# A hybrid decoder block on one core: routing beside the mix product, expert weights in loads of 4 MiB, and a rotation over 16 places

## The chip, the cores and the metric

The kernel runs on one core of a Trainium2 chip. The metric is device time in microseconds (us) for one execution, lower being better; what is compared are medians of several executions. The profiled execution is one more, and it has a time of its own.

## The reference, cut to what matters

A token mixer (a gated convolution beside chunked retention, 16 meta tokens ahead of 256 real ones) is followed by a mixture of experts: 32 experts, 4 for each token. `EXPERT_BLOCK` is only how the reference pads; each expert has 8 MiB of `w_gate_up` and 4 MiB of `w_down` in float32.

```python
h = h + token_mixer(rmsnorm(h, norm_mix_w), ...)      # ends in: merged @ w_mix_out
xn = rmsnorm(h, norm_ffn_w)
logits = xn @ w_router + b_router                     # 256 x 32
top_v, top_i = lax.top_k(logits, 4)
gates = softmax(top_v)
def expert(xb, e):                                    # for the tokens that chose e
    hgu = xb @ w_gate_up[e] + b_gate_up[e]            # 1024 -> 2048
    g, u = min(hgu[:, :1024], 7), clip(hgu[:, 1024:], -7, 7)
    return (g * sigmoid(1.702 * g) * (u + 1)) @ w_down[e] + b_down[e]
h = h + sum of gates * expert outputs
out = rmsnorm(h, norm_final_w)[:, 16:]
```

## The kernel before

**Stages.** The five engines run hand-written streams, tied by semaphores; there is no scheduler. Up to about 394 us of the profiled execution the token mixer runs: products with `w_in` in split precision (L500 to L502), with `w_ret_out` (L582) and `w_conv_out` (L484). Then come the product with `w_mix_out` (L605, `yret` times the ring's units), the second norm, the router (L618), and the choice of experts. From 452 us on the experts run, one block of up to 64 token slots at a time; with these inputs there are 32 blocks, one per expert. `last` and `rounds` are read from `nblocks`, a table that DVE works out (`further_blocks`).

**Routing before.** The mix product goes through its four column units `n`, with both token halves `t` in each. As each pair of units ends, DVE adds it to the residual `hx`. When all four are in, ACT squares both halves (L906), POOL makes the inverse roots (L438), DVE writes the normed tokens `xn2` (L1226), and TensorE transposes them (L462), ACT copies them from PSUM to `xn2T` (L912), and TensorE multiplies by the router `wr`. DVE takes the maxima, their indices, a mask and (after products with `before` and `ones`) the rank of each token at its expert, in `slot`. The tokens of a block are gathered by a product with a one-hot matrix. That product is in bfloat16; so that nothing is lost, the tokens are split in three parts, `x3` (ACT writes a part, L909, L916, L921; DVE subtracts it and leaves the rest, L1231, L1257). The gather (L634) makes `xT`, the block's tokens with the model dimension on the partitions. Eight products with the identity (L718) put `hx` in PSUM banks 0 to 3, where the experts' outputs are added up.

**A block.** Its weights are 12 units of 1 MiB: eight of `w_gate_up` and four of `w_down`. The order on TensorE is: `hidden(1)` with units 4 to 7 of gate_up, the gather for the next block, the scatter of the block before (L707), `down(0)` with two units of w_down (L683), `hidden(0)` of the next block with its units 0 to 3, `down(1)` with the last two. `hidden` is L662, and L655 is its bias, which comes first. Each unit that has been used adds one to `w_used`: 4 after the first `hidden(0)`, 12 more for each block.

**Loads.** SP issues them all, in one queue. The first four units have places of their own in `split_w` and are never loaded again; the other twelve places (`pair_w`, `rT`, two parts of `ring`, `scratch`) are taken in pairs, 2 MiB for each load, in rows of 16 KB per partition. `pair` (L328) loads one; `reload` waits until both units of the place have been used:

```python
sp.wait_ge(w_used, LOADS * b + (n + AHEAD + 2))
pair(n, e, of, j)
```

In all, 16 MiB are loaded ahead of the first expert product, some of it while the token mixer runs: 6 MiB at 304 us, 2 at 368, and the rest from 396 on; the last pair waits for the router and for `x3`.

## Time and profile before

| | |
|---|---|
| median of 3 executions | 1382.29 us (1381.57 to 1383.05) |
| the profiled execution | 1390.49 us, span 1388.7 us, mean granted clock 0.987 |
| busy share of the span | PE (TensorE) 93%, DVE 39%, ACT 19%, POOL 1% |
| the chain that ended last | PE 51%, DMA 43%, of which rT<-in_w_gate_up 42% |
| moved | 467.78 MB, mean 337 GB/s over the span |

The span runs from the first to the last instruction of the profiled execution. Shares of busy time are means over stages that differ: in the second half of the span all 16 DMA engines are busy as well. PEld is TensorE's loading of weights, which overlaps PE. A float32 product shows as two records.

### The profile page before, as it was taken

Reading aid. Unit: us, or ns where it says so; the run is one execution under the profiler, and the core shown is the slowest. Engines: PE = TensorE matmul, PEld = TensorE weight load, DVE = VectorE, ACT = ScalarE, POOL = GpSimd, SP = SyncE. Lnnn points to the kernel's source line nnn. Section 1 sums busy time; section 2 is a strip of 40 time slices with the busy share of each in tenths; the row PEclk is TensorE's granted clock in tenths of the full one; section 3 lists DMA queues with packets and bytes.
Section 4 is the critical chain, followed back from the end, with each engine's and each line's share of the span. In section 5 each row is a group of like instructions: output and inputs, shape, how many; then the busy total and the mean of one; then the engine's idle time right before and its main releaser. Section 6 shows DMA issues by size and latency. Waiting matters only on the chain.

```text
span 1388.7 us, 21351 instructions
## 1 busy us (share of the span) xinstructions
PE 1292.2 (93%) x8375; PEld 720.2 (52%) x8375; DVE 538.9 (39%) x1070; ACT 260.3 (19%) x468; POOL 13.5 (1%) x29
## 2 busy tenths in 40 slices
PE   4999999999997999999999999999999999999996
PEld 4998899898886334333333333333333333333332
DVE  5797898851214423232322223223222222232231
ACT  5554443420103111111111101101111111011011
POOL 1000000000000000000000000000000000000000
PEclk9999999999997999999999999999999999999998
DMA  9653443456661699999999999999999999999994
GB/s 305 219 162 122 150 151 130 144 200 225 210 245 61 236 430 429 427 429 429 429 427 429 429 429 428 428 429 429 428 428 429 429 428 429 429 429 428 428 429 201
DMA packets 89374, 467.78 MB, mean 337 GB/s; under 512 B 5647, under 2 KB 63543, under 8 KB 64679
## 3 DMA queue, kind: packets, MB, share of 16 engines
q1 hardware_dynamic: 88112, 465.27, 82.3%
q10 hardware_dynamic: 1239, 2.20, 0.6%
q8 instruction: 14, 0.23, 0.1%
q14 instruction: 9, 0.07, 0.0%
HBM read 466.41 MB, written 1.05 MB: 337 GB/s over the span
## 4 chain that ended last, share of the span: by engine, by line
PE 51%; DMA 43%; DVE 2%; ACT 2%; issue 1%; ACTq 0%; SPq 0%; DVEq 0%; POOL 0%
DMA rT<-in_w_gate_up 42%; PE pb L662 15%; PE pb L500 6%; PE pb L502 6%; PE pb L501 6%; PE pb L683 5%; PE pb L582 4%; PE pb L605 2%; PE pb L484 2%; PE pb L462 1%; ACT ubuf L932 1%; PE pb L618 1%; PE pb L674 1%; PE pb L568 0%; DMA hx<-in_x 0%
## 5 line engine op out<-in xcount | busy, mean ns | idle before, releaser
L683 PE MATMUL pb<-ring,ubuf 128*64 128x512 f32 x1008 | 230.2, 598 | 19.1 <-ACT ubuf L932 14.7
L1346 DVE TENSOR_SCALAR scratch<-pb 64x512 f32<-64x512 f32 x64 | 43.7, 682 | 472.6 <-PE pb L662 472.6
L500 PE MATMUL pb<-parts,whi 128*128 128x256 f32 (+1 forms) x640 | 187.0, 292 | 5.6 <-DVE parts L1005 5.6
L502 PE MATMUL pb<-parts,wlo 128*128 128x256 f32 (+1 forms) x640 | 183.6, 287 | 0.0
L501 PE MATMUL pb<-parts,whi 128*128 128x256 f32 (+1 forms) x640 | 183.6, 287 | 0.0
L662 PE MATMUL pb<-rT,ubuf 128*64 128x512 f32 x512 | 118.2, 604 | 28.4 <-DMA rT<-in_w_gate_up 28.4
L683 PEld LDWEIGHTS pb<-ring,ubuf 128*64 128x64 f32 x1008 | 66.8, 136 | 140.7 <-issue 107.9
L500 PEld LDWEIGHTS pb<-parts,whi 128*128 128x128 f32 x640 | 122.2, 191 | 8.9 <-issue 8.9
L501 PEld LDWEIGHTS pb<-parts,whi 128*128 128x128 f32 x640 | 121.9, 190 | 1.5 <-issue 1.5
L502 PEld LDWEIGHTS pb<-parts,wlo 128*128 128x128 f32 x640 | 122.1, 191 | 0.0
L662 PE MATMUL pb<-pair_w,ubuf 128*64 128x512 f32 x512 | 116.4, 596 | 0.0
L662 PE MATMUL pb<-scratch,ubuf 128*64 128x512 f32 x496 | 111.7, 592 | 0.0
L662 PE MATMUL pb<-ring,ubuf 128*64 128x512 f32 x496 | 111.7, 592 | 0.0
L992 DVE TENSOR_TENSOR wlo<-ring,whi 128x1024 fp32r<-128x1024 f32 x80 | 97.5, 1220 | 22.9 <-ACT whi L806 22.8
L806 ACT ACTIVATE whi<-ring 128x1024 fp32r<-128x1024 f32 x80 | 84.2, 1057 | 108.4 <-PE pb L502 104.8
L1036 DVE SCALAR_TENSOR_TENSOR scratch<-ubuf,par,scratch 128x256 f32<-128x256 f32 x232 | 97.4, 478 | 0.0
L662 PEld LDWEIGHTS pb<-rT,ubuf 128*64 128x64 f32 x512 | 35.1, 138 | 110.0 <-issue 61.3
L928 ACT ACTIVATE scratch<-scratch 64x512 f32<-64x512 f32 x64 | 39.9, 624 | 269.8 <-DVE scratch L1346 269.8
L932 ACT ACTIVATE ubuf<-pb 128x256 f32<-128x256 f32 x64 | 24.6, 384 | 314.0 <-PE pb L672 314.0
L662 PEld LDWEIGHTS pb<-ring,ubuf 128*64 128x64 f32 x496 | 35.6, 137 | 70.8 <-issue 70.8
L662 PEld LDWEIGHTS pb<-pair_w,ubuf 128*64 128x64 f32 x512 | 34.8, 137 | 71.3 <-issue 58.0
L707 PE MATMUL pb<-ubuf 64*128 64x512 f32 x264 | 65.6, 615 | 0.9 <-ACT ubuf L944 0.9
(212 smaller groups left out, 1143.9 us busy)
## 6 DMA issues: line engine op xcount, KB each, us to landing
ring<-in_w_down SPq DMA_DIRECT2D x63, 2048.0 KB, 21.9
pair_w<-in_w_gate_up SPq DMA_DIRECT2D x32, 2048.0 KB, 25.5
rT<-in_w_gate_up SPq DMA_DIRECT2D x32, 2048.0 KB, 25.5
scratch<-in_w_gate_up SPq DMA_DIRECT2D x31, 2048.0 KB, 22.7
ring<-in_w_gate_up SPq DMA_DIRECT2D x31, 2048.0 KB, 24.1
ring<-in_w_in SPq DMA_DIRECT2D x40, 1024.0 KB, 5.1
ring<-in_w_ret_out SPq DMA_DIRECT2D x8, 1024.0 KB, 5.0
split_w<-in_w_gate_up SPq DMA_DIRECT2D x2, 2048.0 KB, 10.1
```

Source lines behind the costliest of these rows:

```text
L500: pe.matmul(o, wh, xh, start=first, stop=False)
L501: pe.matmul(o, wh, xl, start=False, stop=False)
L502: ins = pe.matmul(o, wl, xh, start=False, stop=last)
L582: ins = pe.matmul(pb[:, 2 * (f % 2) + j, 0:REAL], ring[:, s, k % KC, j * P:(j + 1) * P], rT[:, VC + k, :], start=(k == 0), stop=(k == 2 * ...
L662: ins = pe.matmul(pb[u * SLOTS:(u + 1) * SLOTS, bank, :], xT[:, 2 * i + k, :], w[:, k, u * HID:(u + 1) * HID], start=False, stop=(i == 3 a ...
L683: ins = pe.matmul(pb[c * SLOTS:(c + 1) * SLOTS, 6, :], actT[:, s, 2 * i + k, :], w[:, k, c * HID:(c + 1) * HID], start=False, stop=(s == 1 ...
L707: ins = pe.matmul(pb[:, 2 * t + c, :], hotT[rows, t * P:(t + 1) * P], ysb[rows, :], start=False, stop=stop, skip_group_check=True)
L806: sc.activation(whi[:, 2 * (u % 2) + c, :], m_raw(u, c), ACT.Copy).then_inc(m_hi, 1)
L928: sc.activation(sig, hg, ACT.Sigmoid, scale=ALPHA).then_inc(sig_rdy, 1)
L992: dve.tensor_tensor(wlo[:, 2 * (u % 2) + c, :], m_raw(u, c), whi[:, 2 * (u % 2) + c, :].bitcast(F32), ALU.subtract).then_inc(m_lo, 1)
L1036: ins = dve.scalar_tensor_tensor(out=acc if w < TAPS - 1 else cv[:, 2 * i + j, :], in0=u, scalar=tap, in1=acc, op0=ALU.mult, op1=ALU.add)
L1346: dve.tensor_scalar(hg, pb[0:SLOTS, 4 + s, :], LIMIT, None, ALU.min).then_inc(min_rdy, 1)
```

## The change

There are two parts.

**The routing.** The mix product now goes through the first token half for all four units, and then through the second. While it is at the second half, the first is added to the residual, multiplied by the norm's weight (into a new buffer `hw`, without the inverse root), transposed, and multiplied by the router; the inverse root is applied to the logits instead. The choice for the first half is made there as well. The first block's gather no longer uses the three bfloat16 parts: it is a float32 product of `hw` with `hot1`, for each half, into banks 5 and 7. The three parts, the identity products and the block table are still made, and stand behind the first block's gather.

On TensorE, at the end of the mix product, before (each pair of rows is one token half; L462 the transposes, L618 the router, L624 to L628 the ranks, L634 the gather, L718 the identity products, L655 the first expert product's bias):

```order
L605 MATMUL pb<-ring,ubuf 128x256 x15
L462 MATMUL pb<-ident,ubuf 128x128 [waits xn_done]
...
L462 MATMUL pb<-ident,ubuf 128x128 [waits xn_done]
...
L618 MATMUL pb<-scratch,ring 128x32 [waits x2e,rout_in]
...
L618 MATMUL pb<-scratch,ring 128x32 [waits x2e]
...
L624 MATMUL pb<-scratch,before 128x32 [waits lgt_read,route]
...
L634 MATMUL pb<-onehot,scratch 128x64 [waits hot_rdy,x3_rdy]
L634 MATMUL pb<-onehot,scratch 128x64 x47
L718 MATMUL pb<-hx,ident 128x512 [waits h2_done]
L718 MATMUL pb<-hx,ident 128x512 x3
...
L655 MATMUL pb<-bias,pick_e 64x512 [waits xt_rdy,sel_rdy,zeroed,b3_step]
```

And now, from the transposes of the first half on (L475 transposes, L644 the mix product, L620 the router, L657 and L666 ranks, L630 the float32 gather, L706 the bias):

```order
L475 MATMUL pb<-ident,hw 128x128 [waits hw_done]
...
L644 MATMUL pb<-work,ubuf 128x256 [waits landed4]
...
L620 MATMUL pb<-work 128x32 [waits x2e,rout_in]
...
L620 MATMUL pb<-work 128x32 [waits x2e]
...
L644 MATMUL pb<-work,ubuf 128x256 [waits landed5]
...
L657 MATMUL pb<-work,before 128x32 [waits h2_done,route]
L475 MATMUL pb<-ident,hw 128x128 [waits hw_done]
...
L620 MATMUL pb<-work 128x32 [waits x2e]
...
L630 MATMUL pb<-hot,hw 128x64 [waits hot_rdy,xf_rdy]
...
L630 MATMUL pb<-hot,hw 128x64 [waits hot_rdy,xf_rdy]
...
L706 MATMUL pb<-bias,pick_e 64x512 [waits xt_rdy,sel_rdy,zeroed,b3_step]
```

The transposes and the router of the first half stand ahead of the mix product's last unit; the three-part gather and the identity products are gone from ahead of L706. They stand right behind the first four units instead:

```order
L713 MATMUL pb<-split_w,ubuf 64x512 [waits e_in0]
...
L713 MATMUL pb<-split_w,ubuf 64x512 [waits e_in0]
L713 MATMUL pb<-split_w,ubuf 64x512 x3
L772 MATMUL pb<-hx,ident 128x512 [waits h2_done,table_done]
L772 MATMUL pb<-hx,ident 128x512 x3
L775 TENSOR_LOAD nblocks [waits x3_rdy]
L775 ISA x2
L776 TENSOR_LOAD nblocks
L776 ISA x2
...
L706 MATMUL pb<-bias,pick_e 64x512 [waits clip_rdy,min_rdy]
```

Before, L727's load of `last` followed there alone. Now two waits, the identity products (L772) and two register loads stand between the first `hidden(0)` and block 0's `hidden(1)`, whose bias is the last row.

On DVE, in what it does between the second rank and the first block's tokens, before (L1257 subtracts the second part, L1259 is `slot`, L1262 the one-hot, L1298 writes `xT`):

```order
L1254 TENSOR_REDUCE scratch<-scratch 128x32 [waits route_step]
L1257 TENSOR_TENSOR ring<-ring,scratch 128x2048 [waits x3_rdy]
L1259 SCALAR_TENSOR_TENSOR scratch<-pb,scratch 128x64 [waits rank_done]
L1262 TENSOR_SCALAR onehot<-iota_s,scratch 128x64 [waits route_step]
L1262 TENSOR_SCALAR onehot<-iota_s,scratch 128x64
...
L1303 MEMSET scratch 64x512 [waits gathered]
L1304 MEMSET scratch 64x512
L1298 COPY ubuf<-pb 128x512 [waits gathered]
...
L1269 TENSOR_SCALAR scratch<-pb 128x32
```

And now (L1393 and L1396 write `xT`, L1405 subtracts a part, L1359 begins the block table):

```order
L1321 TENSOR_REDUCE work<-work 128x32 [waits route_step]
L1327 SCALAR_TENSOR_TENSOR work<-pb,work 128x32 [waits rank_done,route]
L1329 TENSOR_SCALAR hot<-iota_s,work 128x64 [waits route_step]
...
L1393 COPY ubuf<-pb 128x512 [waits first_done]
L1396 TENSOR_TENSOR ubuf<-ubuf,pb 128x512 [waits gathered,half_done]
L1397 MEMSET work 64x512
L1398 MEMSET work 64x512
...
L1405 TENSOR_TENSOR hw<-hw,work 128x2048 [waits x3_rdy]
L1359 TENSOR_SCALAR work<-pb 128x32 [waits rank_done]
...
L1379 MEMSET off 128x32 [waits route_step]
L1405 TENSOR_TENSOR hw<-hw,work 128x2048 [waits xr_rdy,x3_rdy,route_step]
```

The subtractions of 2048 columns have moved behind `xT`, with the block table between them.

**The loads.** The parts of SBUF are laid out anew, so that 16 places of 1 MiB lie in four groups of four in a row. For the first 28 blocks (`FIXED`; expert and block have the same number there) the weights are loaded by `four`, 4 MiB at once, as 128 rows of 32 KB, and all four groups rotate, those of the first units too. The layout of the weights in memory is changed on the host to match. The last blocks are loaded in pairs of 2 MiB, as before, in the upper twelve places. TensorE's loop over blocks is written out four times, since the groups rotate by three for each block.

In SP's queue the first four loads of 4 MiB stand where the mixer still runs (at r = 3 and n = 2 of the loops over the ring's units), behind the merge, and behind the mix product. The fifth waits for four used units; the ones that follow wait for 8, 16, 14, 20, 28, 26, ... used units, in this order.

The core of the diff:

```diff
+            def four(i, e):
+
+                b = (i - 1) // 3
+                of, q, d = ((w_gu, 0, 0), (w_gu, 1, 0), (w_dn, 0, 0))[i % 3] if i else (w_gu, 0, 0)
+                x = e + (b + 1 if i % 3 == 0 else b) if i else 0
+                sp.dma_start(place_at(4 * (i % 4), 4), expert_src(x, of, q)).then_inc(e_in[i % 4], 16)
+
+            def used(i):
+
+                b = (i - 1) // 3
+                return LOADS * b + (14, 8, 16)[i % 3] if i else AHEAD
...
             sp.wait_ge(merged, KC)
+            four(2, 0)
+            sp.wait_ge(mix_done, 8)
+            four(3, 0)
...
+            sp.wait_ge(w_used, used(0))
+            four(4, 0)
+            with sp.Fori(0, trips) as g:
+                for i in range(5, 17):
+                    sp.wait_ge(w_used, 4 * LOADS * g + used(i - 4))
+                    four(i, 4 * g)
...
             def reload(b, n, e, of, j):
-                sp.wait_ge(w_used, LOADS * b + (n + AHEAD + 2))
-                pair(n, e, of, j)
+                sp.wait_ge(w_used, LOADS * b + (AHEAD + (FIXED - 1) * LOADS + max(n + 2, 12 if n == 8 else 0)))
+                later_pair(n, e, of, j)
...
+            hidden(0, first_unit, 0)
+            pe.wait_ge(table_done, 4)
             pe.wait_ge(h2_done, 4)
             for t in range(TT):
                 for c in range(2):
                     pe.matmul(pb[:, 2 * t + c, :], ident[:, :], hx[:, t, c * 512:(c + 1) * 512],
                               start=True, stop=False, skip_group_check=True)
+            pe.wait_ge(x3_rdy, PARTS + 1)
...
-    gu = w_gate_up[0].reshape(NE, 2, 2, 2, P, 2, 2, HID).transpose(0, 6, 1, 4, 2, 3, 5, 7).reshape(NE, 4, P, 4 * D)
-    dn = w_down[0].reshape(NE, 2, 2, 2, P, D).transpose(0, 1, 4, 2, 3, 5).reshape(NE, 2, P, 4 * D)
+    gu = w_gate_up[0].reshape(NE, 8, P, 2, 2, HID).transpose(0, 4, 2, 1, 3, 5).reshape(NE, 2, P, 8 * D)
+    dn = w_down[0].reshape(NE, 8, P, D).transpose(0, 2, 1, 3).reshape(NE, 1, P, 8 * D)
```

## Rows read from the trace of the kernel before

**Rows 1.** The page's second part: GB/s moved, in 40 equal slices of the span
```profile
GB/s 305 219 162 122 150 151 130 144 200 225 210 245 61 236 430 429 427 429 429 429 427 429 429 429 428 428 429 429 428 428 429 429 428 429 429 429 428 428 429 201
```

**Rows 2.** Two stretches: us, busy by engine, granted clock, DMA share, GB/s
```profile
25.00:45.00 20.00, 20.00 (x146) 20.00 (x145) 12.84 (x15) 7.87 (x11) 0.00 (x0) 1.00 1.09 348
500.00:1350.00 850.00, 795.49 (x5161) 308.07 (x5157) 227.30 (x471) 92.29 (x234) 0.00 (x0) 1.00 1.01 429
```

**Rows 3.** The chain that ended last, late: start us, us, what
```profile
1304.63 25.49 DMA rT<-in_w_gate_up
...
1330.16 3.68 PE pb L662 x16
...
1333.99 26.19 DMA rT<-in_w_gate_up
```

**Rows 4.** SP's queue, expert loads of 2 MiB: start us, us, instruction
```profile
444.87 0.34 SPq L328 DMA_DIRECT2D ring<-in_w_down  x1
463.02 0.35 SPq L328 DMA_DIRECT2D pair_w<-in_w_gate_up  x1
466.43 0.34 SPq L328 DMA_DIRECT2D rT<-in_w_gate_up  x1
474.96 0.33 SPq L328 DMA_DIRECT2D ring<-in_w_down  x1
...
487.15 0.33 SPq L328 DMA_DIRECT2D ring<-in_w_down  x1
...
494.23 0.33 SPq L328 DMA_DIRECT2D rT<-in_w_gate_up  x1
```

**Rows 5.** The chain between the mix product and the experts
```profile
438.84 0.20 DVE scratch L1244
...
440.62 2.21 DVE ring L1257
442.85 1.92 ACT scratch L921
...
447.56 4.40 PE pb L718 x8
451.96 0.34 PE pb L655 x2
...
459.16 0.22 PE pb L655 x2
```

**Rows 6.** TensorE in order of time; in brackets the idle time before
```profile
395.55 27.89 PE L605 MATMUL pb<-ring,ubuf 128*128 128x256 f32 x128 [1.03 <-DVE ubuf L1216]
...
427.97 0.89 PEld L462 LDWEIGHTS pb<-ident,ubuf 128*128 128x128 f32 x8 [4.92 <-DVE ubuf L1226]
427.97 1.28 PE L462 MATMUL pb<-ident,ubuf 128*128 128x128 f32 x8 [4.52 <-DVE ubuf L1226]
```

**Rows 7.** DVE and ACT by line and shape: busy us, mean ns, idle before
```profile
L1220 DVE TENSOR_TENSOR hx<-hx,pb 128x512 f32<-128x512 f32 x4 | 2.8, 688 | 25.9 <-PE pb L605 25.9
...
L912 ACT ACTIVATE ring<-pb 128x1024 f32<-128x1024 f32 x2 | 2.0, 1014 | 0.1
```

**Rows 8.** DVE around the block table, in order of time
```profile
447.72 0.48 DVE L1303 MEMSET scratch<- 64x512 f32 x1 [3.61 <-PE pb L634]
...
450.03 0.12 DVE L1269 TENSOR_SCALAR scratch<-pb 128x32 f32<-128x32 f32 x1
...
454.65 0.09 DVE L1289 MEMSET off<- 128x32 f32 x1
```

**Rows 9.** SP reading a register from SBUF: duration ns min/median/max
```profile
L385 SPq TENSOR_LOAD <-nblocks x1: 471/471/471, 452.9 to 452.9; - x1
```

**Rows 10.** A stretch of the router products, columns as in rows 2
```profile
432.15:435.57 3.42, 3.42 (x18) 3.42 (x18) 0.99 (x2) 3.04 (x3) 0.00 (x0) 0.50 0.00 0
```

**Rows 11.** The page's sixth part: KB each, us from issue to landing
```profile
ring<-in_w_in SPq DMA_DIRECT2D x40, 1024.0 KB, 5.1
ring<-in_w_ret_out SPq DMA_DIRECT2D x8, 1024.0 KB, 5.0
```

More of the change, by code:

```diff
@@ L42 @@
 AHEAD = 4
+PLACES = 16
+FIXED = 28
 HW = KC * UNIT // 2
@@ L352, in _ @@
                     sp.wait_ge(b_full, RET0)
-                    for n in range(0, AHEAD, 2):
-                        first_pair(n)
-                    pair(0, 0, w_gu, 4)
+                    four(0, 0)
                 load(LRET + 2 * r, w_ro[:, 0:KC, :], r)
@@ L363, in _ @@
                     sp.wait_ge(b_full, CONV0)
-                    pair(2, 0, w_gu, 6)
+                    four(1, 0)
                 load(LMIX + n, w_mo, n)
@@ L604, in _ @@
+            pe.wait_ge(a_free, 50)
+            for t in range(TT):
+                if t:
+                    pe.wait_ge(b_free, 50)
+                for n in range(UC):
+                    s, use = place(LMIX + n)
+                    pe.wait_ge(landed[s], 16 * use)
                     for k in range(KC):
-                        ins = pe.matmul(pb[:, n, t * UNIT:(t + 1) * UNIT], yret[:, k, t * P:(t + 1) * P],
+                        if t == 0 and n == 0 and k in (0, KC - 2):
+                            pe.wait_ge(merged, KC if k else KC - 2)
+                        ins = pe.matmul(pb[:, 2 * t + n // 2, n % 2 * UNIT:(n % 2 + 1) * UNIT], yret[:, k, t * P:(t + 1) * P],
@@ new lines, in _ @@
+            pe.matmul(pb[:, 0, 0:NE], before[:, :], mask[:, 0, :], start=True, stop=True).then_inc(rank_done, 1)
+            for half in range(2):
+                turn_h2(1, half)
+            pe.wait_ge(lgt_read, 1)
+            for half in range(2):
+                router(1, half)
+            gather_first(0, 5).then_inc(first_done, 1)
+            pe.matmul(pb[:, 1, 0:NE], ones[:, :], mask[:, 0, :], start=True, stop=False)
+            pe.wait_ge(route, 2)
+            pe.matmul(pb[:, 1, 0:NE], before[:, :], mask[:, 1, :], start=False, stop=True).then_inc(rank_done, 1)
```

346 lines of the change are left out of this document (195 added, 151 removed).

## The prediction

> **What bounds the kernel now.** Read first the rate of the weight loads over the span, slice by slice. From the second third on it stands at 427 to 430 GB/s and never moves [rows 1]; over 850 us the DMA engines are all busy, at 429 GB/s [rows 2]. Of the 32 experts' 384 MiB (12 MiB each: 402.7 MB), 16 MiB are fetched ahead of the first expert product and 368 MiB after it: 385.9 MB at 429 GB/s are 900 us. Then read the chain that ended last near its end: in each block it is a transfer of 25.5 us, some products of L662 (3.68), and the next transfer [rows 3]. A block takes 29.36 us there (1304.63 to 1333.99), which is 12.58 MB at 429 GB/s. Thirdly the queue of SP: early on, where TensorE sets the pace, the same place is loaded again after 27.80 us (466.43 to 494.23) [rows 4]. So TensorE needs 27.8 us a block, the loads 29.35, and the experts are bound by the loads once TensorE has used up what was fetched ahead. A TensorE saving within the experts is worth nothing; what counts is when the stream starts to run without a hole, and its rate.
>
> When does it start? The last load ahead is issued at 444.87 and is done some 5 us later; the next is issued at 463.02, as the sixth unit has been used [rows 4]. Two loads (2 MiB, 4.89 us each at 429 GB/s) fit between 463.02 and 474.96, where the next is issued; from there on each is issued before the one ahead of it is through. I call V the moment at which an unbroken stream would have had to begin: V = 474.96 - 2 x 4.89 = 465.2. The latency from issue to the first byte is the same in both kernels and drops out. The end of the kernel moves as V moves.
>
> **The routing.** Between the mix product's end at 423.44 [rows 6] and the first expert product's bias at 451.96 lie 28.5 us of chain: residual, squares, norm, transposes, router (L618), selection, a three-part copy of the tokens (2.21 on DVE at 440.62, 1.92 on ACT at 442.85), gather, and 4.4 us of identity products (L718) [rows 5]. The change puts half of it beside the product and takes out the rest, as the two orders show. Step by step:
> - The product (27.9 us from 395.55) starts when the convolution's last product is done and no longer waits for the last two `merged` chunks: the 1.03 us of idle ahead of it go [rows 6]. Into it go 8 transposes of the first token half (8 took 1.28 us at the full clock [rows 6]) and its 8 router products, 16 records. A load of 128x128 weights took 0.89/8 = 0.11 us [rows 6], so 1.8 us. End of the product: 423.4 - 1.0 + 1.3 + 1.8 = 425.5.
> - Behind it stay, for the second half only: residual of 512 columns 0.69 [rows 7] and the norm's weight at 512 columns, a quarter of L1257's 2.21 over 2048 [rows 5], 0.6; four transposes 0.6; ACT's copy of 512 columns, half of L912's 1.01 [rows 7], 0.5; four router products 0.9; the selection 1.6 (438.84 to 440.62 with one small operation moved out [rows 5]); rank and one-hot 0.8; eight float32 gather products, 16 records, 1.8; an add from PSUM 0.7; some 0.6 of semaphores. Sum 8.8: the first expert product at 434.3, 17.7 us earlier.
> - That is not yet the gain. Three things that stood ahead of the first product now stand behind it. The identity products come after it, and with them a wait for `x3_rdy`, that is for the three-part copy, and two register loads. The copy hangs on DVE: from 434.2 four memsets (0.48 or less each [rows 8]), a subtraction over 2048 columns (2.2 [rows 5]), the block table (450.03 to 454.74, 4.7 [rows 8]), a second subtraction 2.2, then ACT's last part 1.9 [rows 5], and 0.5 of semaphores: 434.2 + 1.8 + 2.2 + 4.7 + 2.2 + 1.9 + 0.5 = 447.5. The product of four units (6.9) and the identities (4.4) are done at 446, so TensorE waits. The two register loads took SP 0.47 and about 0.3, with checks 1.2 [rows 9]. So the second group of hidden products starts at 448.8. Queued behind it: everything of block 0, and through `w_used` the loads.
> - The clock. In the routing of before the granted clock was 0.50, with TensorE busy for a whole stretch on router products of 32 columns [rows 10]. The same thin products now stand in a tighter row. At half clock the router half and the gather (24 records) cost up to 24 x 0.11 = 2.6 more; if it stays full, nothing. I take 1.2: 450.0 against 459.16 before, 9.2 us earlier.
>
> **The loads.** 4 MiB at a time, 9.78 us each. SP waits for the first four units (441.5 to 445), one load; for eight units (457), one load, 9.8 us: through by 468. The third waits until the down units of block 0 are all used, as the group of four is freed only whole, 28.0 us after 450.0 (459.16 to 487.15 [rows 4, 5]): 478.0; the fourth goes with it. So the stream has a hole of some 10 us that it did not have in this size, and two loads of 4 MiB stand ahead of it. V' = 478.0 - 2 x 9.78 = 458.4. V moves by **-6.8 us**: of 17.7 us won in the routing, 8.5 go to what moved behind the first product, 2.4 to the coarser groups.
>
> Does it run dry later? The next group of the first half is freed at 478.0 + 7.1 and the queue lasts until 497.6; the next down group at 478.0 + 27.8 = 505.8, the queue lasts until 507.4 (it was given three loads): 1.6 us to spare, less the latency of an issue, and 1.5 more with each block. Once TensorE waits for loads, it waits for the next block's first group; it then frees the down group 12.2 us later (474.96 to 487.15 [rows 4]), with 19.6 us of loads behind: 7 us to spare. No second hole.
>
> **The rows.** At 25 to 45 us the loads had rows of 1 KB and ran at 348 GB/s with a busy share of 1.09; the experts' rows of 16 KB run at 429 with 1.01 [rows 2]. Per row an engine takes 16 x 1024 / (348/1.09) = 51 ns and 16 x 16384 / (429/1.01) = 617 ns; a straight line through both gives 14 ns per row and 603 per 16 KB. A row of 32 KB would then save 14 of 1234, 1.2%. 81 of the loads have it (340 MB, 792 us): 9.4 us. Rows of 1 KB may be slow for other reasons, and then the saving is nothing. I take half, **-4.8 us**. The Trainium skill, DMA: Bandwidth & Descriptors, section Bandwidth (Where 436 GB/s comes from), puts the fabric at 435 GB/s; by that alone the stream could gain at most 1.4%, and the 429 here agree with it as a ceiling.
>
> **The end.** The last four blocks are loaded in pairs as before. With lumps TensorE starts block 28's second pair of hidden units 12.2 + 3.4 = 15.6 us after the lump, they land 9.8 after it: 5.8 late. It wins back 1.55 in each of three blocks: **+1.1 us** remain. From the last load that TensorE waits for (1333.99 + 26.19) on, the tail is the same [rows 3].
>
> Sum -6.8 - 4.8 + 1.1 = -10.5 us. The profiled execution took 1390.49 with a span of 1388.7, 8.2 more than the median; the change in us carries over: 1382.3 - 10.5 = **1371.8**. The dense part up to 394 has the same instructions on TensorE, DVE and ACT, and no wait of TensorE for a load there; 4 MiB in place of 6 stand in the queue at 304.
>
> **Rivals.**
> 1. As above, the rows of 32 KB giving between 2 and 9 us: 1365 to 1376. Chance 0.50.
> 2. A row costs by its bytes alone. The line through two loads of unlike source and state is thin evidence. Then -5.7: 1376.6. Chance 0.25.
> 3. The first half of block 0 starts later than 450, by the clock falling through the first expert products too or by waits that I did not see in the chain of DVE and ACT. Each us costs one. From 456 on only the rows are left, near the time of before: 1379 to 1385. For it speaks how much the sum joins end to end; against it that the parts are all measured. Chance 0.15.
> 4. Slower: rows 32 KB apart lower the rate at which HBM delivers. 1% of 792 us is 7.9 us, so with nothing gained per row it decides from 1.1% (5.7 + 2.8 us); at 3% the time is 1400. Against it: the loads of w_in, with rows 40 KB apart, landed in 5.1 us, those of w_ret_out, 4 KB apart, in 5.0 [rows 11]. A 7 us margin at the down groups that is really used up would look the same. Chance 0.10. The Trainium skill, DMA: Bandwidth & Descriptors, section Latency and other measured facts, has copies slow down with row pitches that are large powers of two, from 512 KiB on; whether 32 KB rows come near it no run here shows.
>
> **The numbers.** A measurement of this kernel tells 0.2% (2.8 us) from no change. Best: clock full, 9.4 for the rows: -17, 1365. Bound of the others: block 0 at 453, rows nothing: -2.5, 1380. Range 1364.5 to 1380.0, which leaves out most of rival 4 and half of rival 3. Faster 0.84, same 0.06, slower 0.10.
>
> **What would show it.** In the profile after: the first L713 product at 434 to 437; a wait of TensorE for ACT (the copy to x3) ahead of the second group of hidden products, which starts near 450; one hole in the loads, some 10 us, ending near 478, and none after; a rate over 500 to 1250 of 430 to 433 GB/s (429: rival 2; less: rival 4); TensorE waiting for `split_w`, `late_w` or `work` loads once a block, from block 5 or so on. It would be wrong if the hole comes back in each block, or if TensorE's block takes over 29 us.

## The result, and the profile after

| | median, us | range, executions |
|---|---|---|
| before, beside it | 1382.76 | 1381.57 to 1386.55, 5 |
| changed | 1375.12 | 1374.32 to 1377.90, 5 |
| ratio | 0.9949 | 95% interval 0.9931 to 0.9966 |

The change is 7.6 us faster; in a later set, with its own executions of before beside it, 1376.17 against 1382.28 us, ratio 0.9958 (0.9938 to 0.9978). The forecast was 1371.8, 10.5 us faster, with a range of 1364.5 to 1380.0. The profiled execution of the changed kernel took 1375.12 us, its own median.

The page after: span, TensorE, GB/s in 40 slices, and the shares of the chain that ended last.
```profile
span 1373.1 us, 20662 instructions
PE 1282.8 (93%) x8359; PEld 719.0 (52%) x8359; DVE 540.5 (39%) x1075; ACT 262.6 (19%) x474; POOL 12.6 (1%) x29
GB/s 305 218 171 125 150 153 124 153 214 154 214 250 153 256 431 431 430 436 428 431 433 433 429 432 436 429 431 431 436 428 431 434 432 429 432 434 425 427 428 210
PE 63%; DMA 32%; ACT 2%; DVE 1%; issue 1%; ACTq 0%; SPq 0%; DVEq 0%
```
Against [rows 1] the plateau is some 3 GB/s higher, and the chain has moved from DMA (43%) to TensorE (51% to 63%): the last block that waits for a load ends that wait at 1247.66 us (1230.35 + 17.31 below), where in before it was at 1360.18 (1333.99 + 26.19 [rows 3]). The late chain after (start us, us, what):
```profile
1201.21 17.29 DMA late_w<-in_w_gate_up
1218.55 7.09 PE pb L713 x32
...
1226.65 3.68 PE pb L734 x16
1230.35 17.31 DMA split_w<-in_w_gate_up
1247.70 7.09 PE pb L713 x32
```
A block takes 1230.35 - 1201.21 = 29.14 us while the loads bound it, 29.36 before.

The product and the routing on TensorE after (start us, us, instruction, in brackets the idle time before):
```profile
417.52 3.70 PE L644 MATMUL pb<-work,ubuf 128*128 128x256 f32 x16
...
423.34 1.94 PE L620 MATMUL pb<-work 128*128 128x32 f32 x16
...
428.25 3.64 PE L630 MATMUL pb<-hot,hw 128*128 128x64 f32 x16 [0.74 <-DVE hot L1329]
...
433.32 0.64 PE L706 MATMUL pb<-bias,pick_e 128*64 128x512 bf16 x2 [0.62 <-DVE ubuf L1396]
433.72 9.08 PE L713 MATMUL pb<-split_w,ubuf 128*64 128x512 f32 x32
442.73 3.70 PE L772 MATMUL pb<-hx,ident 128*128 128x512 f32 x8
447.93 0.41 PE L706 MATMUL pb<-bias,pick_e 128*64 128x512 bf16 x2 [1.50 <-issue]
```
SP's queue of expert loads after, 4 MiB each:
```profile
300.81 0.34 SPq L327 DMA_DIRECT2D split_w<-in_w_gate_up  x1
...
442.83 0.33 SPq L327 DMA_DIRECT2D split_w<-in_w_gate_up  x1
455.42 0.35 SPq L327 DMA_DIRECT2D late_w<-in_w_down  x1
476.11 0.93 SPq L327 DMA_DIRECT2D work<-in_w_gate_up  x2
483.18 0.33 SPq L327 DMA_DIRECT2D split_w<-in_w_down  x1
503.92 0.33 SPq L327 DMA_DIRECT2D late_w<-in_w_gate_up  x1
```
Four stretches after (us, busy by engine, granted clock, DMA share, GB/s): the hole, the steady part, TensorE's clock in the routing, and an early one.
```profile
467.00:476.00 9.00, 8.53 (x45) 2.98 (x43) 2.74 (x4) 0.93 (x3) 0.00 (x0) 1.00 0.02 5
500.00:1250.00 750.00, 697.99 (x4551) 272.95 (x4553) 201.67 (x415) 81.87 (x208) 0.00 (x0) 1.00 1.00 432
427.60:437.80 10.20, 8.92 (x32) 5.90 (x34) 6.50 (x15) 1.19 (x5) 0.00 (x0) 0.50 0.48 208
21.00:28.00 7.00, 3.69 (x16) 3.70 (x17) 6.60 (x6) 4.21 (x4) 0.00 (x0) 0.53 1.07 338
```

**Two traces must be laid side by side with care.** The spans differ by 15.6 us, the medians by 7.6. The first expert load left SP's queue at 300.81 us here and at 304.39 in before, though nothing ahead of it on TensorE was changed. In before the granted clock was at half in these stretches, inside the long products:
```profile
118.00:121.50 3.50, 3.50 (x6) 1.42 (x7) 0.02 (x1) 0.00 (x0) 0.00 (x0) 0.52 0.90 298
254.70:258.10 3.40, 3.40 (x7) 1.50 (x6) 0.26 (x1) 0.00 (x0) 0.00 (x0) 0.50 0.89 299
```
After, it was at half (1.2 GHz instead of 2.4) at 21 to 28 us instead, where TensorE was busy for 3.69 of 7.0 us. Two times 3.4 us at half cost 3.4; that is the 3.58. It is not the change that did it: later traces of the changed dense part show both forms (the table below). So I add 3.58 us to every time of the changed trace before I set it against before's. What is left of 15.6 is 12.0 us: the start of the stream 4.9, its rate 5.7 (5.9 by the blocks), the rest 1.4.

All traces, by where the granted clock was at half ahead of 400 us, by the start of the first expert load, by the time at half clock in the routing, and by the span that is left behind the first expert load (all us):

| run | half clock ahead of 400 | first expert load | half clock in the routing | span behind that load |
|---|---|---|---|---|
| `before` | near 118 and 255 | 304.39 | 20.5 | 1084.3 |
| `before_again` | near 118 and 255 | 304.67 | 20.5 | 1084.9 |
| `before_third` | 20 to 31, near 164 | 303.26 | 17.1 | 1083.3 |
| changed | 21 to 28 | 300.81 | 10.2 | 1072.3 |
| `after_again` | 20 to 28 | 299.97 | 10.2 | 1072.2 |
| `pairs12` | 20 to 28 | 300.06 | 10.2 | 1076.6 |
| `rows16` | near 118 and 255 | 304.22 | 13.7 | 1080.1 |
| `rows8` | none | 300.47 | 17.1 | 1092.6 |
| `x3late` | near 118 and 255 | 304.38 | 13.7 | 1072.0 |
| `half6` | 20 to 28 | 299.86 | 10.2 | 1070.7 |
| `half6_x3late` | none | 300.58 | 17.1 | 1072.2 |
| `half3_x3late` | 21 to 29 | 300.97 | 10.2 | 1068.0 |
| `warm` | 20 to 28 | 300.10 | 10.2 | 1073.0 |
| `two_loads_32k` | 20 to 28 | 300.09 | 10.2 | 1899.1 |

The last column takes out the dense part, but not the clock in the routing.

### The profile page after: what moved, and what is told of

Read it like the earlier page. It is cut to its first block, busy times and chain, and to the rows that moved or that the text cites. A ratio compares the mean times of both kernels' runs of the same rounds, so it can differ in the third digit from the quotient of the medians.

```text
span 1373.1 us, 20662 instructions
## 1 busy us (share of the span) xinstructions
PE 1282.8 (93%) x8359; PEld 719.0 (52%) x8359; DVE 540.5 (39%) x1075; ACT 262.6 (19%) x474; POOL 12.6 (1%) x29
## 4 chain that ended last, share of the span: by engine, by line
PE 63%; DMA 32%; ACT 2%; DVE 1%; issue 1%; ACTq 0%; SPq 0%; DVEq 0%
PE pb L713 20%; DMA work<-in_w_gate_up 15%; PE pb L734 10%; DMA split_w<-in_w_gate_up 9%; DMA late_w<-in_w_gate_up 7%; PE pb L513 6%; PE pb L515 6%; PE pb L514 6%; PE pb L595 4%; PE pb L644 2%; PE pb L497 2%; ACT ubuf L1006 1%; PE pb L725 1%; PE pb L475 1%; PE pb L723 1%
## 5 line engine op out<-in xcount | busy, mean ns | idle before, releaser
L713 PE MATMUL pb<-work,ubuf 128*64 128x512 f32 x992 | 218.7, 593 | 13.3 <-DMA work<-in_w_gate_up 13.3
L1445 DVE TENSOR_SCALAR work<-pb 64x512 f32<-64x512 f32 x64 | 43.7, 683 | 467.3 <-PE pb L713 467.3
L713 PEld LDWEIGHTS pb<-work,ubuf 128*64 128x64 f32 x992 | 70.2, 137 | 147.4 <-issue 128.3
L734 PE MATMUL pb<-work,ubuf 128*64 128x512 f32 x576 | 131.5, 598 | 11.0 <-ACT ubuf L1006 8.5
L713 PE MATMUL pb<-late_w,ubuf 128*64 128x512 f32 x576 | 127.0, 593 | 6.2 <-DMA late_w<-in_w_gate_up 6.2
L713 PE MATMUL pb<-split_w,ubuf 128*64 128x512 f32 x480 | 107.9, 603 | 7.2 <-DMA split_w<-in_w_gate_up 7.2
L1066 DVE TENSOR_TENSOR wlo<-work,whi 128x1024 fp32r<-128x1024 f32 x80 | 97.5, 1221 | 21.8 <-ACT whi L861 21.8
L861 ACT ACTIVATE whi<-work 128x1024 fp32r<-128x1024 f32 x80 | 84.2, 1056 | 104.5 <-PE pb L515 100.8
L1110 DVE SCALAR_TENSOR_TENSOR work<-ubuf,par,work 128x256 f32<-128x256 f32 x232 | 97.4, 479 | 0.0
L713 PEld LDWEIGHTS pb<-late_w,ubuf 128*64 128x64 f32 x576 | 41.3, 137 | 83.9 <-issue 74.7
L1002 ACT ACTIVATE work<-work 64x512 f32<-64x512 f32 x64 | 39.9, 624 | 229.0 <-DVE work L1445 229.0
L734 PEld LDWEIGHTS pb<-work,ubuf 128*64 128x64 f32 x576 | 38.2, 136 | 80.5 <-issue 61.7
```

What stands on the lines that cost most here:

```text
L713: ins = pe.matmul(pb[u * SLOTS:(u + 1) * SLOTS, bank, :], xT[:, 2 * i + k, :], w[:, k, u * HID:(u + 1) * HID], start=False, stop=(i == 3 a ...
L734: ins = pe.matmul(pb[c * SLOTS:(c + 1) * SLOTS, 6, :], actT[:, s, 2 * i + k, :], w[:, k, c * HID:(c + 1) * HID], start=False, stop=(s == 1 ...
L861: sc.activation(whi[:, 2 * (u % 2) + c, :], m_raw(u, c), ACT.Copy).then_inc(m_hi, 1)
L1002: sc.activation(sig, hg, ACT.Sigmoid, scale=ALPHA).then_inc(sig_rdy, 1)
L1066: dve.tensor_tensor(wlo[:, 2 * (u % 2) + c, :], m_raw(u, c), whi[:, 2 * (u % 2) + c, :].bitcast(F32), ALU.subtract).then_inc(m_lo, 1)
L1110: ins = dve.scalar_tensor_tensor(out=acc if w < TAPS - 1 else cv[:, 2 * i + j, :], in0=u, scalar=tap, in1=acc, op0=ALU.mult, op1=ALU.add)
```

## The experiments

Each is an edit of the changed kernel unless said otherwise. The medians of before that ran with them: 1382.85 (first four), 1382.28 (second four), 1384.54 (`half3_x3late`, `before_third`), 1382.46 (last two). The executions of one kernel lie up to 6 or 10 us apart, and most medians here are of 5 to 12 of them; where two variants of the changed kernel differ by 1 to 3 us and their intervals overlap, the medians alone do not show the difference, and the traces have to.

**before_again.** The kernel before, with no edit.

> The kernel before, unchanged, profiled a second time. In the prediction's trace it took 1390.5 us, 8 over its median, while the changed kernel's profiled time is its median. Theory: the first trace was an unlucky execution (start of the clock, one fall of the clock in the tail, a slightly slower stream), and this one has a span near 1380.5 with the same chain between the mix product and the experts (28.5 us) and a stream of 429 to 430 GB/s. Rival: the profile itself costs this kernel 8 us, and the span is again 1388 or so; then the difference of the two traces (15.6 us) has to be explained by the change. Time against before: 1.000 within 0.002.

Median 1384.0 (1381.29 to 1391.31), ratio 1.0004 (0.9985 to 1.0023). The profiled execution took 1391.31 us, span 1389.6, clock 0.987, falls at the same places. So the theory failed, and the first trace was no single accident: a trace of before again lies some 7 us over the median. Such times occur without a trace as well: of the 70 executions of before that ran beside the variants, 8 took 1388.4 us or more. But all three that were profiled did (with `before_third` below), so the rival, that the profile itself lengthens this kernel, is not refuted.

**rows16.** Each 4 MiB in two loads of 128 rows of 16 KB, same places, same moments.
```diff
-sp.dma_start(place_at(4 * (i % 4), 4), expert_src(x, of, q)).then_inc(e_in[i % 4], 16)
+for c in range(2):
+    sp.dma_start(place_at(4 * (i % 4) + 2 * c, 2),
+                 expert_src(x, of, q)[:, c * 4 * D:(c + 1) * 4 * D]).then_inc(e_in[i % 4], 16)
```

> The changed kernel with each load of 4 MiB issued as two of 2 MiB, rows of 16 KB, into the same places, released and waited for as before in fours. Only the length of the rows and the number of issues differ. Theory (a row costs a fixed part): the stream falls back from 432 to 429 GB/s, a block from 29.14 to 29.36 us, and the kernel takes 5.5 to 6 us longer than the changed one: 1380.5 to 1381, ratio to before 0.9985 to 0.9995. Rival (rows cost by bytes, the faster stream comes from something else, as fewer issues in flight or other places): no difference from the changed kernel, 1375, ratio 0.995.

Median 1383.05 (1379.89 to 1386.23), ratio 0.9984 (0.9969 to 1.0000): the whole gain is gone, 6.9 to 7.9 us over the changed kernel where 5.5 to 6 were expected. A block takes 29.36 us again. In the traces the span behind the first load is 7.8 us longer: 5.9 are the 27 blocks, and its third load of the stream (481.63 us) comes 2.1 us later against the first, in a routing with 13.7 us at half clock in place of 10.2. Its window and, beside it, that of `rows8` below:
```profile
500.00:1250.00 750.00, 693.82 (x4527) 271.17 (x4525) 198.99 (x407) 81.35 (x205) 0.00 (x0) 1.00 1.01 428
```
```profile
500.00:1250.00 750.00, 682.23 (x4433) 266.36 (x4431) 197.54 (x404) 80.45 (x203) 0.00 (x0) 1.00 1.01 422
```

**pairs12.** The new routing with the old loads (2 MiB, 12 places, each pair freed by itself).
```diff
-FIXED = 28
+FIXED = 1
...
-four(2, 0)
+later_pair(4, 0, w_dn, 0)
+later_pair(6, 1, w_gu, 0)
...
-max(n + 2, 12 if n == 8 else 0)
+(n + 2)
```

> The changed kernel's routing with the old scheme of loads: pairs of 2 MiB, rows of 16 KB, twelve places, the first four units loaded once; TensorE's loop is not written out. Theory: the stream starts sooner as pairs are released after 2 units (V = start of the second hidden group + 15.9 - 9.8 us = 454 in the changed kernel's trace, against 456.6 there), 2.6 us won, and the rows lose 5.8: 3 us over the changed kernel, 1378, ratio 0.9970, with the hole of 10 us in the loads gone. Rival (the loads in fours cost nothing at the start, since the routing sets the end): 6 us over, 1381.

Median 1378.7 (1375.76 to 1381.12), ratio 0.9954 (0.9939 to 0.9970), at 429 GB/s and without a hole behind the first loads. So in the medians the routing alone is worth 4.1 us; new places and coarse release with 16 KB rows take it back (1378.7 to 1383.05, +4.4); the long rows and fewer loads give 6.9 to 7.9 (1383.05 to 1376.17 or 1375.12). In the traces, behind the first load, the routing alone is worth 7.7 us (1084.3 to 1076.6), and the step to the changed kernel 4.3.

**x3late.** The wait for the copy `x3` goes from ahead of the second hidden group into the gather behind it.
```diff
-pe.wait_ge(x3_rdy, PARTS + 1)
 rounds = pe.value_load(...)
...
 if more:
+    pe.wait_ge(x3_rdy, PARTS + 1)
     pe.wait_ge(hot_rdy, 2 * b + 4)
     gather()
```

> The changed kernel with the wait for the three-part copy moved from ahead of block 0's second hidden group to the gather that reads it. Theory: 1.5 us of idle of TensorE ahead of that group go, or what of it is not the two register loads (1.0 us at least is the loads by SP's durations, so 0.5 to 1.5), the third load of the stream is issued that much sooner, and the end comes 0.5 to 1.5 us sooner: 1374, ratio 0.994. Rival: the copy is then late at the gather, one product group later, and nothing is won: 1375. Either is near the bound of what can be told by time; the trace tells it.

Median 1373.98 (1372.43 to 1378.42), ratio 0.9924 (0.9901 to 0.9948), 1.1 us below the changed kernel, which the overlapping intervals do not show as a gain. The idle time ahead of the second group is gone; TensorE and ACT's copy, then SP's first load and two early stretches, of that trace:
```profile
447.81 3.70 PE L772 MATMUL pb<-hx,ident 128*128 128x512 f32 x8
451.44 0.41 PE L706 MATMUL pb<-bias,pick_e 128*64 128x512 bf16 x2
449.91 1.91 ACT L995 ACTIVATE work<-hw 128x2048 bf16<-128x2048 f32 x1 [5.09 <-DVE hw L1405]
```
```profile
304.38 0.34 SPq L327 DMA_DIRECT2D split_w<-in_w_gate_up  x1
```
```profile
118.00:121.50 3.50, 3.50 (x6) 1.46 (x7) 0.00 (x0) 0.00 (x0) 0.00 (x0) 0.52 0.94 298
254.50:257.90 3.40, 3.40 (x5) 1.34 (x5) 0.00 (x0) 0.00 (x0) 0.00 (x0) 0.51 0.92 305
```
The load's row is before's 304.39 again, in a kernel with the changed code: with the falls near 118 and 254 us it starts when before's does.

The second group starts at 451.44, before the copy ends (449.91 + 1.91 = 451.82). `rows16`, with the same falls of the clock and the wait where the change has it, starts it at 453.45:
```profile
453.45 0.41 PE L708 MATMUL pb<-bias,pick_e 128*64 128x512 bf16 x2 [2.02 <-issue]
```
So the wait for the copy was real; with the register loads behind it it costs 2.0 us there. Against the first trace of the changed kernel nothing is won (451.44, and 447.93 + 3.58 = 451.51), since in `x3late` the clock was at half for 13.7 us instead of 10.2.

**after_again.** No edit.

> This is the changed kernel without an edit, for a second trace and its own median beside the next three. Theory: its median is 1375 us again (1373.5 to 1377). The profiled executions of the kernel before both had spans of 1388.7 and 1389.6 us while its median is 1382.85; theory: these two executions met more falls of TensorE's clock (mean granted clock 0.987 there, 0.991 to 0.993 in most others), so a trace of the changed kernel that meets the falls near 118 and 255 us will start the mix product about 3.6 us later than its first trace (near 394.5 instead of 390.9), and its span will be longer by about that (1376 to 1378), with a stream rate between 500 and 1250 us of 432 GB/s as in the first trace. Rival: the difference of 3.6 us in the start of the dense part comes from the changed kernel itself; then the mix product starts near 390.9 again, whatever the falls.

Median 1376.17 (1374.14 to 1380.80), as expected. Its trace met the clock's fall near 20 us, not those near 118 and 255, and its first load left at 299.97, so it could not show the late start; the rows of `x3late` above did, and speak against the rival. The span was 1372.2, not 1376 to 1378.

**half6.** One 4 MiB load, the first unit of block 2, as two halves, each sent when its own places are free.
```diff
+for c, n in ((0, 10), (1, 16)):
+    sp.wait_ge(w_used, n)
+    sp.dma_start(place_at(8 + 2 * c, 2), expert_src(2, w_gu, 0)[:, c * 4 * D:(c + 1) * 4 * D]
+                 ).then_inc((e_half, e_in[2])[c], 16)
```

> The changed kernel with one load changed: the first unit of block 2 is taken as two loads of 2 MB, the first sent when 10 of TensorE's units are used, the second at 16, where the changed kernel sends all 4 MB at 16. Nothing else moves. Theory (the hole of some 9 us in the loads near 467 to 476 us is time that the stream never gets back, since the loads bound the kernel from block 2 to block 27): half of the load fills the hole, 2 MB take 4.86 us at 432 GB/s, and the kernel is faster by about 4.9 us than the changed one, median near 1370.3. Rival 1: what holds the stream is TensorE's release of the places after the hole, so that all later loads go out when they did; no change, 1375. Rival 2: the rows of 16 KB of this one load and the queue's extra entry cost more than they bring; over 1376.

Median 1373.11 (1372.69 to 1376.53), ratio 0.9937 (0.9919 to 0.9955): 3.1 us below `after_again`, 2.0 below the first set, with intervals that overlap; not 4.9. Behind the first load its span is 1.5 us shorter than that of `after_again`, with the same half clock. SP's queue, then two stretches of it and of `after_again`:
```profile
463.06 12.53 SPq L394 DMA_DIRECT2D work<-in_w_gate_up  x2
476.02 0.35 SPq L328 DMA_DIRECT2D work<-in_w_gate_up  x1
482.48 0.34 SPq L328 DMA_DIRECT2D split_w<-in_w_down  x1
503.22 0.33 SPq L328 DMA_DIRECT2D late_w<-in_w_gate_up  x1
```
```profile
466.00:475.50 9.50, 9.03 (x47) 3.24 (x45) 2.74 (x4) 1.13 (x3) 0.00 (x0) 1.00 0.52 215
500.00:508.00 8.00, 8.00 (x42) 2.69 (x38) 1.23 (x2) 0.78 (x2) 0.00 (x0) 1.00 0.68 258
```
```profile
466.00:475.50 9.50, 9.03 (x47) 3.15 (x45) 2.74 (x4) 0.95 (x3) 0.00 (x0) 1.00 0.02 5
500.00:508.00 8.00, 8.00 (x42) 2.73 (x40) 1.36 (x2) 0.78 (x3) 0.00 (x0) 1.00 1.04 451
```
Half of the first hole is filled (5 to 215 GB/s), and a new one opens at 500 to 508 (451 to 258 GB/s), since the load issued at 503 waits for TensorE as before. Both stand in the trace: the theory was right on the hole and wrong on how much of the lead is kept. In the changed kernel three loads issued at 476.11 last until 476.11 + 3 x 9.71 = 505.24, and the next was issued at 503.92: 1.3 us to spare, and about as much of the lead was kept.

**half6_x3late.** Both edits.

> The changed kernel with two edits: the split load of the run before, and the wait for the third part of the router's input moved from ahead of the second hidden group to the gather behind it (alone, the latter gave a median of 1373.98, 1.1 us below the changed kernel). Theory: the two gains are of different pieces of the start (the split load fills a hole, the moved wait takes away 1.5 us of idle TensorE ahead of the releases), so they add: 4.9 + 1.1 = 6.0 us, median near 1369.1. Rival: with the hole filled the stream is held by the release of another place, which the moved wait shifts as well or not at all; then the pair gives no more than the better of the two, 1370.3, or 1374 if the split load gives nothing.

Median 1371.59 (1371.06 to 1374.90), ratio 0.9919 (0.9902 to 0.9937): 1.5 below `half6`, with intervals that overlap. Its trace does not show the gain: behind the first load its span is that of the changed kernel, 1072.2 us, and its load behind the hole was issued at 478.12 us, 1.4 us later against the first than in `half6`, in a routing with 17.1 us at half clock in place of 10.2. That the two gains add is not shown by this run.

**half3_x3late.** As before, with the first units of blocks 2, 3 and 4 halved.
```diff
+if i % 3:
+    ...
+else:
+    for c in range(2):
+        sp.wait_ge(w_used, used(i - 4) - (6, 0)[c])
+        sp.dma_start(place_at(4 * (i % 4) + 2 * c, 2),
+                     expert_src(i // 3, w_gu, 0)[:, c * 4 * D:(c + 1) * 4 * D]
+                     ).then_inc((e_half[i // 3 - 2], e_in[i % 4])[c], 16)
```

> The changed kernel with the moved wait of the router's input and three split loads in place of one: the first unit of blocks 2, 3 and 4 is taken as two loads of 2 MB, each half sent when its own places are free. With one split load the hole of 10.9 us in the stream near 467 to 479 us shrank to 5.8, but a new one of 3.7 us opened near 503, since the next load of 4 MB still went out at 503.2 us. Theory (a lead in the stream is kept only as far as the later releases allow: TensorE frees a block's places every 27.9 us and the loads take 29.1, so the release at 503 has 1.3 us to spare, the one at 531 has 2.5, the one at 559 has 3.8): with three split loads the hole of 503 is filled too, the lead is cut to 3.8 us near 559 instead of 1.3 near 503, and the kernel is 2.0 to 2.5 us faster than the one with one split load: about 2 us below its median of 1371.6, so 1369.4. Rival: the lead is lost elsewhere (the extra 16 KB rows, or the end, where TensorE is the bound); then 1371.6 again.

Median 1368.39 (1367.40 to 1374.28), ratio 0.9890 (0.9866 to 0.9915): the fastest kernel here, 1.1% under before and some 7 us under the changed one; its interval lies apart from those of the changed kernel. Behind the first load its span is 4.2 us shorter than that of `after_again` and 2.7 shorter than that of `half6`, all three with 10.2 us at half clock in the routing. Its queue and stretches:
```profile
481.74 0.33 SPq L328 DMA_DIRECT2D split_w<-in_w_down  x1
490.26 12.52 SPq L397 DMA_DIRECT2D late_w<-in_w_gate_up  x2
502.83 0.43 SPq L328 DMA_DIRECT2D work<-in_w_gate_up  x1
```
```profile
500.00:508.00 8.00, 8.00 (x40) 2.70 (x38) 0.68 (x1) 0.78 (x2) 0.00 (x0) 1.00 0.97 414
558.00:562.00 4.00, 4.00 (x22) 1.37 (x20) 0.00 (x0) 0.78 (x2) 0.00 (x0) 1.00 0.88 320
```
The hole at 503 is closed (414 GB/s), and a small one stands at 558 to 562, where the theory put the next limit.

**warm.** Three filler products of the identity, to keep TensorE's clock up.
```diff
+for _ in range(2):
+    pe.matmul(pb[:, 5, :], ident[:, :], hx[:, 0, 0:512], start=True, stop=True)
 turn_h2(1, 1)
...
+for _ in range(1):
+    pe.matmul(pb[:, 3, :], ident[:, :], hx[:, 0, 0:512], start=True, stop=True)
 pe.wait_ge(xt_rdy, 1)
```

> The changed kernel with three matmuls of the identity against 512 columns that nobody reads, two of them between the last two groups of transposes of the router's input and one ahead of the wait for the router's scores. They leave the output as it is. Theory: TensorE's clock falls to half near 427 us because TensorE does thin or no work while the routing of the first blocks waits for other engines; if the filler keeps the granted clock at full, the second gather takes 1.81 us instead of 3.66 and the first hidden group 6.87 instead of 8.84, in all 3.9 us, against 0.2 us for each of three matmuls on the way: faster by about 3 us, near 1372. Rival: three matmuls are too little to alter the clock; no change or up to 1.4 us slower, 1375 to 1376.5, with the same stretch at half clock in the trace.

Median 1375.16 (1375.07 to 1378.85), ratio 0.9949 (0.9931 to 0.9967): no change. The clock was at half just as long:
```profile
426.60:436.80 10.20, 9.46 (x35) 6.54 (x36) 5.50 (x12) 1.34 (x5) 0.00 (x0) 0.50 0.48 208
```
What would keep it up was not found.

**before_third.** The kernel before once more.

> The kernel before, unchanged, for a third trace. The first two had spans of 1388.7 and 1389.6 us, clock falls near 118 and 255 us, a half-clock stretch of 20.5 us from 429 us, and a mean clock of 0.987; its median time is 1382.8. Theory: that stretch in other executions is 10 to 14 us, as in all traces of the changed kernel and its variants, and its stream of expert loads then starts 3 to 5 us earlier against the mix product, so that the routing and the new places are worth less in the medians than in the two traces. If this trace is of that kind: the mix product near 390, the stretch of 10 to 14 us from about 425 us, the load behind the first hidden group near 436 to 440 us instead of 444.9, span 1379 to 1383. If it is of the first kind again, nothing is told apart.

Median 1383.37 (1381.34 to 1390.97), ratio 0.9999 (0.9978 to 1.0019); profiled 1388.4 us, span 1386.6, clock 0.986. Its product, two stretches and the first load with a place freed by block 0:
```profile
394.42 27.89 PE L605 MATMUL pb<-ring,ubuf 128*128 128x256 f32 x128 [1.03 <-DVE ubuf L1216]
```
```profile
426.20:429.60 3.40, 2.76 (x13) 2.60 (x14) 1.87 (x2) 2.11 (x3) 1.00 (x1) 0.50 0.00 0
433.00:446.70 13.70, 10.03 (x74) 8.33 (x74) 8.28 (x26) 4.66 (x7) 0.00 (x0) 0.50 0.32 105
```
```profile
460.11 0.35 SPq L328 DMA_DIRECT2D pair_w<-in_w_gate_up  x1
```
From the product's start to that load: 460.11 - 394.42 = 65.7 us; in the first trace 463.02 - 395.55 = 67.5 [rows 4, 6]. With 17.1 us at half clock in place of 20.5 (428.7 to 449.2) before's stream starts 1.8 us sooner. The direction is as the theory has it. Its "10 to 14 us, as in all traces" of the variants is wrong: `half6_x3late` had 17.1, and so has `rows8`. An execution of before with 10 to 14 us at half was not caught in a trace.

**two_loads_32k.** Each 4 MiB in two loads of 64 rows of 32 KB (upper and lower partitions).
```diff
+for c in range(2):
+    sp.dma_start(place_at(4 * (i % 4), 4)[64 * c:64 * c + 64], expert_src(x, of, q)[64 * c:64 * c + 64]
+                 ).then_inc(e_in[i % 4], 16)
```

> The changed kernel with each load of 4 MB given as two loads of 2 MB of 64 rows of 32 KB (the upper and the lower half of the partitions) into the same places at the same time. The run with two loads of 128 rows of 16 KB had a stream of 428.4 GB/s between 500 and 1250 us and was 6.9 us slower than the changed kernel (1383.05 against 1376.2), but it changed both the length of the rows and the number of loads. Theory (the length of the rows sets it): rows of 32 KB again, so 431.5 GB/s and 1376 us. Rival (it is the number of loads and of their entries in the queue): 428.4 GB/s and 1383 us. Second rival: 64 rows at a time use half of the queues' width or of the memory's ports at a time, and the stream is slower than either, below 425 GB/s and above 1390 us.

Median 2193.88 (2177.79 to 2201.91), ratio 1.5846 (1.5794 to 1.5898):
```profile
500.00:1250.00 750.00, 421.22 (x2169) 150.20 (x2171) 96.24 (x196) 39.70 (x100) 0.00 (x0) 0.77 1.00 209
```
The stream runs at 209 GB/s with a busy share of 1.00: less than half of 432. The second rival, far beyond its size. The Trainium skill, SBUF — State Buffer, section Door 1: The DMA port swizzle, has a load of 64 partitions reach 8 of the 16 ports, up to 218 GB/s, and the section "Can I just issue two DMAs to hit both halves?" answers no. Both agree with the 209 here. So this run does not tell the length of the rows from the number of loads.

**rows8.** Each 4 MiB in four loads of 128 rows of 8 KB.

> The changed kernel with each load of 4 MB given as four loads of 1 MB of 128 rows of 8 KB into the same places at the same time. Theory (each row costs its bytes and a fixed part): a block of 12 MB took 29.14 us with rows of 32 KB (24 rows for each of the 16 DMA engines) and 29.36 with 16 KB (48 rows), so 9 ns a row; with rows of 8 KB (96) a block takes 29.36 + 48 x 0.009 = 29.80 us, a stream of 422 GB/s, and 27 blocks add 17.8 us to the changed kernel's 1376: 1394. Rival (there is no fixed part, the pairs of loads were slower since they share the queue): the stream does not fall with the rows by that step; 428 GB/s and 1383 us, as with two loads. Second rival: 8 KB rows cross a bound of their own and fall further, below 415 GB/s.

Median 1394.87 (1391.70 to 1398.62), ratio 1.0079 (1.0057 to 1.0102), 422 GB/s: forecast 1394 and 422. A block takes 29.82 us (TensorE's waits end on loads issued 29.82 us apart, 1191.31 to 1221.13), forecast 29.80. The three rates, 432, 428 and 422, follow 9 ns for each row. The count of loads doubles with the rows in both steps, so what is shown is that the cost grows in proportion to one of the two. A stretch of before speaks for the rows: the loads of `w_in` are of 1 MiB like those of `rows8`, but of rows of 1 KB, and ran at 348 GB/s [rows 2]. That is 3.01 us for 1 MiB against 2.48, with 64 rows for each DMA engine against 8: 9.4 ns for each row more, at the same size of load. It is another stage and another source, so it supports the reading and does not prove it.

## Why the prediction was near, and where it was off

The range held the time and the likeliest case came out; the sum was 3 to 4 us too large. Some of that is luck: in the traces the start gave less than forecast and the rows and the end more, and in the medians the start gave nothing. By its steps (times of the changed trace with 3.58 added):

- **End of the product**, 425.5: 421.22 + 3.58 = 424.8 (417.52 + 3.70). Right; the routing of the first half does hide in the product. The 1.28 us for eight transposes were not all at the full clock, which fell at 428.7 us, inside them; at full clock eight took 1.04.
- **First expert product**, 434.3: 433.32 + 3.58 = 436.9. 2.6 late. The second half's float32 gather took 3.64 us instead of 1.8, as the clock was at half from 427.6 to 437.8. The step on the clock had up to 2.6 more on the thin products and took 1.2.
- **The first hidden group** took 9.08, not the 6.9 that the step assumed: the clock was still at half. The identities took 3.70, not 4.4. TensorE then waited 1.50 us for `x3` and the registers; forecast as a wait until 448.8. The second hidden group started at 447.93 + 3.58 = 451.5, forecast 450.0. `x3late` and `rows16` confirm the wait and its cause, the copy.
- **The hole** of some 10 us ending near 478: loads 3 and 4 went out at 476.11 + 3.58 = 479.7; the stream moved 5 GB/s from 467 to 476. V' = 479.7 - 2 x 9.71 = 460.3 against 465.2: -4.9 where -6.8 stood. `pairs12` bears the measure out: the `w_down` load that before issued at 474.96 us went out at 462.50 there, with the first load at 300.06 instead of 304.39; that is 8.1 us sooner, and its span is 7.7 shorter. No hole opened later in the changed kernel, as forecast. The spare time at the next down group was 1.3 us, as thin as forecast (1.6 us at 505.8). `half6` shows what that means: a lead brought forward by 4.9 us is cut there; the spare time grows by 29.14 - 27.8 = 1.3 us with each block.
- **The rows**, -4.8 with 0 and -9.4 as bounds: 27 blocks x (29.36 - 29.14) = 5.9 by the chain, 5.7 by the rates of 428.4 (`rows16`) and 431.5 GB/s. Half of the bound was a choice between 0 and 9.4, not a working, so that it came near is luck in part. A row costs 9 ns, if the rows are what counts, where the straight line gave 14. That line went through rates divided by the busy shares 1.09 and 1.01. Through the plain rates, 16 x 1024 / 348 = 47 ns and 16 x 16384 / 429 = 611 ns for each row, it gives 9.5 ns, 6.1 us for the 81 loads, and 422 GB/s for rows of 8 KB, which is what `rows8` measured. (14 of 1234 is 1.1%, 9.0 us, not the 9.4 that the sum had.) The Trainium skill's ceiling of 435 GB/s (DMA: Bandwidth & Descriptors, Where 436 GB/s comes from) was not passed over 750 us: 432; single slices of the profile's page, 34 us long, read up to 436.
- **The end**, +1.1: it came out at about -1.4, as the remainder of 12.0 - 4.9 - 5.7. TensorE was the bound from 1247.66 on, over four blocks from the end, and in before's trace the last stretch still had its wait for loads. This term was argued on the wrong side; no run isolates it.
- **"The change in us carries over"** from the profiled execution to the median. This is the step that failed. In the traces the change is worth 12.0 us by the alignment, more than the 10.5; in the medians 6.1 to 7.6. The profiled 1390.49 us was 8.2 over its median, and the prediction took this surplus as a constant that drops out. All three traces of before came from executions of 1388.4 to 1391.3 us with a mean clock of 0.986 or 0.987, 5.0 to 8.2 over their medians, while the two of the changed kernel lie at theirs or 2 below. The medians say which term shrinks: the routing gives 4.1 (`pairs12`), where the sum had 9.2 and the aligned traces show 7.7 (459.16 to 451.5 for the second hidden group, and the same 7.7 for the span of `pairs12`). `before_third` shows 1.8 us of that difference as less time at half clock in before's own routing. With the 4.4 that the coarse release takes, nothing is left in the medians of the start's -6.8; the 6.1 to 7.6 us come with the long rows and fewer loads. The two variants that were caught with the clock's falls near 118 and 255 us, `rows16` and `x3late`, lie 3.0 and 4.4 us over their medians too, so the dense part, which drops out of the alignment, holds a good part of before's surplus. The remainder is open: an execution of before at its median was never traced, and whether the profile itself lengthens before is not settled.

Of the rivals, 2 (rows by bytes alone) and 4 (slower by the pitch) are refuted by 432 GB/s; 3 was true in part: the first hidden group started 2.6 us late and ran at half clock, and the second started 1.5 us late.

## What to carry to other kernels

When a stream of loads is the bound, a place is worth what the earliest release makes of it: large loads for the steady part (4 MiB in rows of 32 KB instead of 2 MiB in rows of 16 give 0.8% of the rate here) and halved ones only while the consumer still sets the pace; follow a lead forward through the next releases before you count it. Set a change's size in the trace against a trace of the same kind: first check that the unchanged part ahead of it starts at the same time, and check how the profiled execution stands to the median; if it lies above, the stage that holds the difference may be the one that you are about to save.

## What the runs showed that was not expected

- Loads that cover 64 partitions each ran at 209 GB/s against 432 over 128, at the same 32 KB rows and the same total.
- Rows of 32, 16 and 8 KB: 432, 428 and 422 GB/s, in queues that never ran dry.
- TensorE's granted clock fell to 0.50 in the routing in every trace but for different times: 10.2, 13.7 or 17.1 us in the changed kernel and its variants, 17.1 or 20.5 in before. In the changed kernel TensorE was busy for 8.92 of the 10.2 us, with thin products and the first expert products. Three more products of 512 columns altered nothing.
- The clock's falls outside of the routing come at other times from execution to execution: near 20 us alone, near 118 and 255 us, near 20 and 164 us, or not at all. With the falls near 118 and 255 us the first expert load goes out at 304.22 to 304.67 us, with none or the one near 20 at 299.86 to 300.97. The routing's time at half clock goes with the form: in the changed kernel and its variants 10.2 us in all seven traces with the fall near 20, 13.7 in the two with those near 118 and 255, 17.1 in the two with none.
